# An unused 160-byte tensor ahead of a 118 KiB scratch area: one start address in on-chip memory

## The reference, cut to what matters

```
def rmsnorm(x, g):
    xf = x.astype(jnp.float32)
    y = xf * lax.rsqrt(jnp.mean(xf * xf, axis=-1, keepdims=True) + EPS)
    return (y * g.astype(jnp.float32)).astype(x.dtype)

def swiglu(x, w_gate, w_up, w_down):
    return (jax.nn.silu(x @ w_gate) * (x @ w_up)) @ w_down
...
        x = x + 0.5 * swiglu(rmsnorm(x, ffn1_norm[l]), ffn1_w_gate[l], ffn1_w_up[l], ffn1_w_down[l])
```

## The kernel before, in words

| tensor | starts at byte, before | above a multiple of 256 |
|---|---|---|
| `raw` | 1152 | 128 |
| `whi` | 25728 | 128 |
| `wlo` | 50304 | 128 |
| `ahi`, `alo` | 74880, 78976 | 128 |
| `x` | 83072 | 128 |
| `con` | 91264 | 128 |
| `vec` | 102784 | 128 |
| `stat` (256 bytes) | 103648 | 224 |
| `arena`, and in its place `f_both` | 103904 | 224 |
| `key_hi`, `key_lo` | 128480, 136672 | 224 |
| `hhi`, `hlo` | 196064, 204256 | 224 |
| `ln_gain` (4096 bytes) | 224736 | 224 |

## Time and profile before

### The profile page before, as it was taken

One profiled execution on the slowest core, in us unless ns is written; L12 is line 12 of the kernel. 1 busy time (PEld: TensorE's weight loads), 2 busy tenths in 40 slices (PEclk: granted clock), 3 DMA queues, 4 the chain that ended last, 5 costly groups with the idle time before them and its releaser, 6 DMA issues.

```text
span 1236.5 us, 23237 instructions
## 1 busy us (share of the span) xinstructions
PE 1221.5 (99%) x9698; PEld 1059.7 (86%) x9698; DVE 538.8 (44%) x819; ACT 608.8 (49%) x796; POOL 776.8 (63%) x200
## 2 busy tenths in 40 slices
PE   8999999999999999999999999999999999999998
PEld 7888887788988888899898888888888998888887
DVE  4432234655333323343523333348986573332233
ACT  7454443545564444585565445464422444554442
POOL 3988880153288888766369888843016525888884
PEclk9999999999999999999999999999999999999999
DMA  7655554244255555554235555542341033555551
GB/s 297 215 186 196 180 201 147 85 178 150 100 176 202 200 177 201 189 184 164 103 137 202 176 200 179 195 170 103 136 162 46 38 112 124 187 194 196 180 201 68
DMA packets 31020, 202.01 MB, mean 163 GB/s; under 512 B 3424, under 2 KB 5344, under 8 KB 7392
## 3 DMA queue, kind: packets, MB, share of 16 engines
q1 hardware_dynamic: 28064, 196.63, 45.1%
q10 hardware_dynamic: 2880, 4.26, 1.0%
HBM read 198.79 MB, written 2.10 MB: 162 GB/s over the span
## 4 chain that ended last, share of the span: by engine, by line
PE 95%; ACT 1%; POOL 1%; issue 1%; DVE 1%; DMA 1%; SPq 0%; POOLq 0%; DVEq 0%; ACTq 0%
PE psum L352 25%; PE psum L354 13%; PE psum L343 10%; PE psum L344 10%; PE psum L345 10%; PE psum L985 6%; PE psum L998 3%; PE psum L2991 2%; PE psum L3007 1%; POOL wlo L3370 1%; PE psum L2846 1%; PE psum L340 1%; PE psum L342 1%; PE psum L341 1%; PE psum L2961 1%
## 5 line engine op out<-in xcount | busy, mean ns | idle before, releaser
L3370 POOL TENSOR_TENSOR wlo<-raw,whi 128x2048 fp32r<-128x2048 f32 x160 | 734.4, 4596 | 291.9 <-ACT whi L313 245.3
L352 PE MATMUL psum<-f_both,whi 128*128 128x512 f32 x1408 | 496.7, 394 | 1.6 <-DVE wlo L698 1.6
L313 ACT ACTIVATE whi<-raw 128x2048 fp32r<-128x2048 f32 x160 | 306.4, 1916 | 223.7 <-PE psum L354 173.2
L354 PE MATMUL psum<-f_both,wlo 128*128 128x256 f32 x1408 | 393.0, 279 | 0.0
L352 PEld LDWEIGHTS psum<-f_both,whi 128*128 128x128 f32 x1408 | 263.9, 187 | 64.6 <-DVE wlo L698 2.1
L354 PEld LDWEIGHTS psum<-f_both,wlo 128*128 128x128 f32 x1408 | 264.1, 188 | 1.5
L343 PE MATMUL psum<-whi,ahi 128*128 128x512 f32 x352 | 137.9, 392 | 0.2 <-POOL wlo L3370 0.2
L344 PE MATMUL psum<-wlo,ahi 128*128 128x512 f32 x352 | 137.7, 391 | 0.0
L345 PE MATMUL psum<-whi,alo 128*128 128x512 f32 x352 | 136.9, 389 | 0.0
L908 DVE TENSOR_TENSOR psum<-psum,arena 128x512 f32<-128x512 f32 x43 | 30.1, 700 | 241.0 <-ACT arena L624 240.9
L924 DVE TENSOR_TENSOR alo<-arena,ahi 128x512 fp32r<-128x512 f32 x44 | 98.8, 2247 | 31.7 <-ACT ahi L857 31.7
(11 more groups left out here) (425 smaller groups left out, 1474.0 us busy)
## 6 DMA issues: line engine op xcount, KB each, us to landing
raw<-stream SPq DMA_DIRECT2D x182, 1024.0 KB, 4.9
con<-consts SPq DMA_DIRECT2D x1, 1376.0 KB, 14.3
x<-x_in SPq DMA_DIRECT2D x1, 1024.0 KB, 5.1
raw<-stream SPq DMA_DIRECT2D x2, 512.0 KB, 7.1
kept_x<-x ACTq DMA_DIRECT2D x1, 1024.0 KB, 3.9
x<-kept_x ACTq DMA_DIRECT2D x2, 512.0 KB, 4.8
out<-x SPq DMA_DIRECT2D x4, 256.0 KB, 2.0
arena<-gm_w_s ACTq DMA_DIRECT2D x1, 512.0 KB
```

The costliest lines, as they stand in the source:

```text
L313: nc.scalar.activation(whi[:, slot, :], raw[:, c % RAW, :], ACT.Copy).then_inc(high_made, 1)
L352: nc.tensor.matmul(psum[:, bank, :].rearrange("p (a n) -> p a n", a=2), whi[w], f_both[:, :, k, :], start=k == 0, stop=False, skip_group_c ...
L354: return nc.tensor.matmul(psum[:, bank, 0:TOK], wlo[w], f_hi[:, k, :], start=False, stop=k == KT - 1, skip_group_check=True)
L3370: nc.gpsimd.tensor_tensor(part(wlo[:, slot, :]), part(raw[:, c % RAW, :]), part(whi[:, slot, :]).bitcast(F32), ALU.subtract)\
```

## The change

One line makes a tensor of 40 float32 columns (160 bytes) that nothing reads or writes:

```diff
         con = sb("con", [P, CONSTS.shape[1]])
         vec = sb("vec", [P, VEC_COLS])
         stat = sb("stat", [P, 64])
+        sb("up_to_line", [P, 40])
         H_AT = 23040
         MORE_AT = H_AT + 2 * KT * TOK
         ARENA = MORE_AT + 3072
```

## The result

Against the 1228 us that I forecast, the changed kernel takes 1240.88 us, the median of six runs (1240.66 to 1243.30); the kernel before takes 1236.53 over its six. The ratio is 1.0033, 95% interval 1.0022 to 1.0043. So the change makes the kernel slower by 0.33%, about 4 us. Both profiled executions lie on that side: their spans are 1236.5 and 1239.1 us. The figure lies within the range that I gave, 1214 to 1246, but on the other side of the time before.

The account below looks back on a forecast made before the run. TensorE, busy 1221.5 of 1236.5 us, was taken as the bound. The profiled 1238.3 us less 8.8 for moving operands, all else 0, gave 1229.5; that execution stood 1.5 above the timed median, hence 1228 us, range 1214 to 1246.

Parts of the forecast that it names:

- the plain products: Plain float32 matmuls (L985, L998 and small ones): whichever operand is in the arena makes no difference, put at 0.
- A: Split matmuls, both operands outside the arena, one moving run of 512 columns: 226.7 ns each, 13.3 lost; must not move.
- term 1: 3128 matmuls with the moving operand in the arena (L352, L354, L340 and sisters): lining up their starts saves 8.8 us.
- B: Moving from `whi`/`wlo`, stationary operand in the arena, 256 columns: 117.2 ns each; forecast to stay.
- C: Moving operand in the arena, stationary outside, 256 columns: 120.0 ns each; forecast to fall to 117.2.
- slower rival: Split matmuls with both starts alike lose 13.3 ns per run: up to 17.2 us more, 1254.0 us; chance 0.21.
- Term 2: Stationary operand in the arena (L343 and sisters), 864 matmuls of 256 columns, 120 of 512: between 4.3 less and 3.1 more, taken as 0.
- no change: Rival: start addresses do not matter in the split matmuls, time stays at 1236.8 us; chance 0.33.
- D: Stationary in the arena, moving two runs of 256 columns from two slots: 234.3 ns each, 21.0 lost, evidence against the forecast.
- in step: TensorE's reads of moving columns and next weights meet when both start alike, chiefly in the L352 and L354 pair.
- The reading of the clock: TensorE's clock was taken to stand at full speed, 2.4 GHz, in all 40 slices of the profile.

Follow-up runs that it names:

- e1: Standalone kernel, computation left out, TensorE alone: 48 matmuls or pairs per combination of operand start offsets; pairs 353.3 ns at 0,0 and 32,32, 346.7 with moving 32 further.
- e7: The changed kernel with 32 more bytes ahead of `raw`, so every tensor stands 32 bytes further at unchanged distances: 1241.25 us, 1.0031 of before.
- e6: The kernel before plus a tensor of 48 columns, putting the arena 32 bytes above the weights modulo 256: 1232.78 us, 0.9957 of before.
- e5: Standalone kernel, TensorE alone: 100 stretches of 32 matmuls or pairs, one operand 0 to 248 bytes above the other modulo 256; pairs 353.5 ns at 64.
- e11: Standalone kernel, TensorE alone: narrower stationary operands, and stretches entered behind 1, 2, 3 or 8 other matmuls; pairs at distance 0 took 346.7 or 353.3 ns.
- e8: e6 with `hhi` and `hlo` 160 bytes further, so 192 above the weights modulo 256: 1229.78 us, 0.9940 of before.
- e2: The kernel before plus a tensor of 24 columns, putting the arena at distance 192: 1239.14 us, 1.0011 of before.
- e3: The kernel before with `hhi` and `hlo` 32 bytes further, at distance 128, the rest of the arena at 96: 1237.78 us, 1.0003 of before.
- e4: The changed kernel with `hhi` and `hlo` 32 bytes further, at distance 32, the rest of the arena at 0: 1240.64 us, 1.0028 of before.
- e9: The changed kernel with a tensor of 104 instead of 40 columns, so the arena starts 256 bytes further: 1241.79 us, 1.0038 of before.
- e10: The kernel before plus a tensor of 80 columns, putting the arena 160 bytes above the weights modulo 256: 1233.49 us, 0.9963 of before.

## Why the prediction was wrong

The bound was read rightly, and so was what does not matter: the plain products, the other engines and the idle time stayed, and A kept its steady 226.7 ns. That a start address has a price, and that it is in the distances between starts, held as well. Then:

- *"If a start that is off costs something in either place and never gains"*, the condition on which term 1 rests. This is the step that failed, with the reading under it that operands are off or on a multiple of 64. e1 shows that both off is as both on, e7 shows it in the full kernel, and e6 shows that an operand 32 off can be the faster one. B and C, from which I took the 2.8 ns, differ because the same 96 bytes lie on different sides (stationary further, or moving further); e5 gives 118.7 and 119.8 for them alone. B's 117.2 was besides only one of its two speeds in the kernel before: with the same operands (555.66 - 545.81) / 83 = 118.7 ns in the rows below this list. From the difference of two sides of one distance nothing follows for a distance of 0.
- Term 1, priced at 8.8 us less with the pair at 344.4: pairs went up by 3.3 ns to 353.3, and the moving operands of 256 columns stayed at 120.0. Together 2.6 us more by the sum over starts. My bounds, 340.0 and 360.0 a pair, held it, and the time lies in my range because the slower rival had a share in it, not by this sum.
- Term 2, priced at 0: `hhi` stationary went to 120.0, 1.7 us more (not 864 x 2.8 = 2.4, since part of B ran at 118.7 before), and two slots to 226.7, 0.7 us less without clock and waits.
- Not in any term: A. Its first nine matmuls behind the pairs take (520.88 - 518.78) / 9 = 233.3 ns (231.1 before), perhaps since it is entered otherwise. With `ahi` and `alo` at the same place, that is 0.9 us more over the kernel.
- The rival *no change* had D for it, which I read as a price of the break between two runs. At distance 0 the two slots take 226.7, like one run of 512: in that steady state there is no price of a break.
- The slower rival came nearest, with the wrong reason and size. It said that a loss of 13.3 ns would fall on each run. It falls on each matmul: 120.0 for 256 columns and 226.7 for 512, in one run or two. By that a pair would be 346.7, and in three stretches of the change and in eight of e11 it is. The cycle of 349, 350 and 361 is 6.7 ns above it, and that I did not foresee. Two reads *in step* as the cause is not shown.
- The reading of the clock was right by the slices, 9 in all 40, but these hide the 3.4 us at half clock. At 1.6 us they would account for the 1.5 us by which the profiled execution stood above the timed runs (an estimate).

Rows of the kernel before, a stretch of `hhi` stationary at B's other speed, 83 matmuls from the first to the second:

```profile
545.81 0.28 PE L343 MATMUL psum<-whi,hhi 128*128 128x256 f32 x1
...
555.66 0.28 PE L345 MATMUL psum<-whi,hlo 128*128 128x256 f32 x1
```

The two pages of the Trainium skill led to "no change", and the measurements decide against both. The 16-byte lines of "SBUF — State Buffer" ("Specifications (TRN2)") do not settle the time: distances of 0, 32, 96 and 192 are all whole lines and give pairs of 353.3, 346.7, 350.0 and 353.3 ns. They may still have a part. In e5 pairs at whole lines take 346.7 to 353.5, and with the moving operand 8 bytes from one 353.3 to 359.9; with the stationary operand 8 bytes further a pair took 347.0 in e1. The page "TensorE: Matmul & The Clock Gate" says in "Step-by-step: what each phase is for" that loading the next tile's weights does not steal read bandwidth from the running matmul. In e11, 64 stationary columns instead of 128 took 256 moving ones from 120.0 to 113.4 ns, and moving the stationary operand alone changes the time of the same matmuls in e1 (119.8 to 118.3). So in these float32r matmuls the two are not independent, though what they share is open.

What stays open: what the two reads share. It is shown that the distance counts, that 256 bytes more leave everything as it was, and that at one distance there can be more than one steady cycle, with the same addresses and another entry. Why is not shown, and the widths of e11 speak against the simple account. I tried no other data type than these float32r matmuls, nor steered the entries in the full kernel.

## What to carry to other kernels

When TensorE is bound by dense float32r matmuls, read the distance from start to start in a steady stretch and compare it with columns / 2.4 GHz; if more than a few ns are lost, sweep the distance between the moving and the stationary tensor with TensorE alone, then choose the paddings from that table. Give each kind of stretch its own distance: here 32 for the gate and up pairs and 192 for the projections made 1229.78 us of 1237.24. Do not argue from "aligned" to "fast", and time again when anything ahead of such a stretch or in front of such a tensor is changed, since 32 bytes or one matmul more can move a stretch by 2%. The table alone does not give the time: it promised 5.2 us for the second distance, and 2 to 3 came.

## What the runs showed of the hardware that was not expected

- At a distance of 0 the steady distance between starts is 120.0 ns for 256 columns and 226.7 for 512, 13.3 over the columns at 2.4 GHz; other steady cycles average 113.3, 117.8, 346.7 and 353.3. 120.0, 226.7, 113.3, 346.7 and 353.3 are whole multiples of 6.67 ns, the time of 16 columns; 117.8, and the 350.0 of a distance of 96, are not.
- Stretches can be in one of two steady speeds 2 to 4% apart at the same addresses (e8, e11), and most stay there to their end, 27 matmuls and more.
- Plain float32 matmuls, which stream half as fast, showed nothing of it: 216 ns from start to start and 1.99 us for eight, at distances of 96 and 0, with either operand in the arena.
- In the trace before, the granted clock stood at half for 3.4 us, from 1.2 us after a wait of 2.08 us, and it cost 1.6 us. The 40 slices of the page do not show it. e2, e3, e4, e6 and e9 have the same wait and such a fall within 1.4 us of its end; the change, e7, e8 and e10 have the wait and no fall there.
